# Adding the experts' results to the residual in another shape, and the final norm tile by tile

## The reference, cut to what matters

```
h = x + mixer(rmsnorm(x))                      # 264 rows x 1024
logits = rmsnorm(h) @ w_router + b_router      # top 4 of 32 experts, softmax gates
h = h + sum over the 4 chosen experts e of
        gate_e * (((clip(up)+1) * glu(gate)) @ w_e2[e] + b_e2[e])
y = h * rsqrt(mean(h*h) + 1e-5) * norm_f       # final norm, the outputs y_prompt and y_sample
```

## Time and profile before

| | us |
| --- | --- |
| median of 3 runs (1486.15 to 1487.38) | 1487.25 |
| the profiled execution, whole | 1487.55 |
| its span, first to last instruction | 1485.8 |
| PE busy | 1382.9 (93%) |
| DVE busy | 374.4 (25%) |
| ACT busy | 228.7 (15%) |
| POOL busy | 96.2 (6%) |

### The profile page before, as it was taken

One profiled execution on the slowest core, in us unless ns is written; L12 is line 12 of the kernel. 1 busy time (PEld: TensorE's weight loads), 2 busy tenths in 40 slices (PEclk: granted clock), 3 DMA queues, 4 the chain that ended last, 5 costly groups with the idle time before them and its releaser, 6 DMA issues.

```text
span 1485.8 us, 17919 instructions
## 1 busy us (share of the span) xinstructions
PE 1382.9 (93%) x7365; PEld 707.5 (48%) x7365; DVE 374.4 (25%) x677; ACT 228.7 (15%) x340; POOL 96.2 (6%) x160
## 2 busy tenths in 40 slices
PE   8999989999999988998999989989999899899996
PEld 7667658778888533332433333324333333233331
DVE  3224332532411332122121221221212212211123
ACT  1122222211000421111101111111011111110102
POOL 1122222210000210000000000000000000000000
PEclk9999999999999999999999999999999999999999
DMA  9788867875243469999999999999999999999993
GB/s 373 293 290 277 289 215 281 291 270 208 114 156 135 180 274 428 412 421 431 414 423 430 412 430 422 428 429 421 425 430 427 428 419 421 430 428 418 430 422 136
DMA packets 52063, 518.48 MB, mean 349 GB/s; under 512 B 6167, under 2 KB 6439, under 8 KB 19742
## 3 DMA queue, kind: packets, MB, share of 16 engines
q1 hardware_dynamic: 37370, 469.09, 75.9%
q0 software_dynamic: 12720, 45.14, 9.0%
q10 hardware_dynamic: 1940, 3.78, 0.7%
HBM read 496.35 MB, written 21.67 MB: 349 GB/s over the span
## 4 chain that ended last, share of the span: by engine, by line
PE 84%; DMA 7%; DVE 4%; ACT 3%; issue 1%; POOL 0%; DVEq 0%; SPq 0%; POOLq 0%; ACTq 0%
PE bank L1544 30%; PE bank L1272 17%; PE bank L1578 15%; PE bank L1589 6%; DMA out_ret_sample<-arena 5%; PE bank L1523 4%; PE bank L1315 3%; PE bank L1409 2%; PE bank L1542 1%; ACT arena L862 1%; PE bank L1570 1%; DMA k_kept<-arena 1%; DVE arena L1212 1%; DVE arena L1223 1%; DVE hx L1227 1%
## 5 line engine op out<-in xcount | busy, mean ns | idle before, releaser
L1544 PE MATMUL bank<-ring,arena 128*64 128x512 f32 x2048 | 444.8, 592 | 0.0
L1272 PE MATMUL bank<-arena,ring 128*128 128x264 f32 x1536 | 350.5, 388 | 0.0
L1272 PEld LDWEIGHTS bank<-arena,ring 128*128 128x128 f32 x1536 | 290.3, 190 | 53.5 <-issue 5.0
L1544 PEld LDWEIGHTS bank<-ring,arena 128*64 128x64 f32 x2048 | 143.7, 137 | 283.0 <-issue 277.3
L1578 PE MATMUL bank<-ring,arena 128*64 128x512 f32 x1024 | 225.1, 592 | 0.0
L1578 PEld LDWEIGHTS bank<-ring,arena 128*64 128x64 f32 x1024 | 71.8, 137 | 131.9 <-issue 129.4
L1212 DVE TENSOR_SCALAR arena<-bank 128x512 f32<-128x512 f32 x32 | 22.1, 692 | 396.5 <-PE bank L1544 396.5
L1589 PE MATMUL bank<-arena 128*128 128x512 f32 (+1 forms) x192 | 91.3, 610 | 12.6 <-DVE arena L1223 12.6
L1523 PE MATMUL bank<-arena 128*128 128x128 bf16 x768 | 61.6, 240 | 31.3 <-DVE arena L1204 31.3
L1223 DVE COPY arena<-bank 64x512 f32<-64x512 f32 x32 | 21.9, 683 | 229.0 <-PE bank L1578 229.0
L1523 PEld LDWEIGHTS bank<-arena 128*128 128x128 bf16 x768 | 56.1, 109 | 46.0 <-issue 46.0
(11 more groups left out here) (198 smaller groups left out, 817.7 us busy)
## 6 DMA issues: line engine op xcount, KB each, us to landing
ring<-in_w_pairs SPq DMA_DIRECT2D x192, 2048.0 KB, 15.2
ring<-in_w_mixer SPq DMA_DIRECT2D x60, 1024.0 KB, 9.1
arena<-in_state_ret POOLq DMA_DIRECT2D x32, 512.0 KB, 6.9
out_ret_sample<-arena POOLq DMA_DIRECT2D x32, 512.0 KB, 6.4
arena<-v_decode POOLq DMA_DIRECT2D x32, 256.0 KB, 8.3
out_ret_prompt<-arena ACTq DMA_DIRECT2D x4, 512.0 KB, 5.3
hx<-in_x_prompt SPq DMA_DIRECT2D x2, 512.0 KB, 3.8
v_kept<-arena ACTq DMA_DIRECT2D x2, 512.0 KB, 9.4
```

The lines of the kernel that those rows point to most:

```text
L1272: ins = pe.matmul(bank[:, 0:T], weight(n + k // 4, k % 4)[:, 128 * j:128 * (j + 1)], rhs[:, k, :], start=k == 0, stop=k == KD * groups - 1)
L1544: ins = pe.matmul(out, xgT[:, k, 64 * e:64 * (e + 1)], held(n, 2 * D * (k % W1_KS) + c), start=False, stop=k == KD - 1)
```

## The change

Decode rows are no longer a third tile of 8 rows x 512 columns, added in two halves. Their 1024 columns lie as four groups of 256, group j in partitions 32j to 32j+7 of a new buffer `hs` (128 x 256, zero elsewhere). In the combine four matmuls, each with 32 stationary columns (8 of rows, 24 of zeros), write partitions 32j to 32j+31 of one bank, and one add of 128 x 256 takes them all. The four prompt matmuls follow, each in a bank of its own: 6 for the decode rows, then 7, 0, 1, 2. No combine matmul waits for an add any more. Waits for `added` stand instead before the gather (first two adds) and before the first products of each expert (first four, all five).

```diff
+ADDS = 5
+ADDED = ADDS - 1
+ADD_BANKS = (6, 7, 0, 1, 2)
+ADD_TILES = ((0, 0), (0, 1), (1, 0), (1, 1))
@@ TensorE, combine
-                    for t, n in enumerate(ROWS):
-                        for c in range(2):
-                            if t:
-                                pe.wait_ge(added, 6 * it + (2 * t + c - 1 + ADDED))
-                            pe.matmul(psum[6 + c][0:n, :], pgT[:, 128 * t:128 * t + n], ysb[:, 512 * c:512 * (c + 1)], ...
+                    for j in range(4):
+                        ins = pe.matmul(psum[ADD_BANKS[0]][32 * j:32 * (j + 1), 0:256], pgT[:, LP:LP + 32],
+                                        ysb[:, 256 * j:256 * (j + 1)], start=True, stop=True)
+                    ins.then_inc(combined, 1)
+                    for n, (t, c) in enumerate(ADD_TILES):
+                        pe.matmul(psum[ADD_BANKS[n + 1]][:, :], pgT[:, 128 * t:128 * (t + 1)], ysb[:, 512 * c:512 * (c + 1)], ...
@@ TensorE, gather and first product
-                    pe.wait_ge(added, 6 * it + ADDED)
+                    pe.wait_ge(added, ADDS * it + 1)
+                        pe.wait_ge(added, ADDS * it + (3 + e))     # for e in range(2)
@@ VectorE, adds
+                    v.tensor_tensor(hs[:, :], hs[:, :], psum[ADD_BANKS[0]][:, 0:256], ALU.add).then_inc(added, 1)
+                    for n, (t, c) in enumerate(ADD_TILES):
+                        v.tensor_tensor(hx[:, t, 512 * c:512 * (c + 1)], ..., psum[ADD_BANKS[n + 1]][:, :], ALU.add)
```

The final norm goes by halves of tiles. ScalarE squares and sums `hs`, then each of the four 128 x 512 pieces as its add completes, adding the halves of a row inside the root:

```diff
+            ac.activation(squares3[:, 4, 0:256], hs[:, :], ACT.Square, accum_out=stat[:, 4:5]).then_inc(hs_squared, 1)
+            for n, (t, c) in enumerate(ADD_TILES):
+                ac.activation(squares3[:, n, :], hx[:, t, ...], ACT.Square, accum_out=stat[:, n:n + 1])
+                if c == 0: Identity(scale=1/D, bias=eps) -> stat[5+t]     # mean3
+                else:      Sqrt(scale=1/D, bias=stat[5+t]) -> stat[8+t]   # root3
+                if n == 1: Sqrt of psum[3][:, 0:1] -> stat[7]             # hs_root
```

More of the change, by code:

```diff
@@ L155, in laid_out_experts, with laid_out_tail @@
     return out
+def laid_out_tail(inputs):
+    p = np.arange(128)
+    same_row = (p[:, None] % 32 == p[None, :] % 32).astype(np.float32)
+    return np.concatenate([same_row, np.repeat(inputs["norm_f"].reshape(4, 256), 32, axis=0)], axis=1)
 PROJ_BANKS = 3
@@ L301, in build @@
         rounds_i = sb("rounds_i", [128, 1], I32)
+        hs = sb("hs", [128, D // 4])
         arena = sb("arena", [128, 21700])
@@ L367, in build @@
         acts = view(4096, 2, 512)
-        squares3 = view(1024, TT, D)
+        squares3 = view(1024, 5, D // 2)
+        y_first = view(17148, D)
         actT = view(5120, 2, 512)
         ysb = view(6144, D)
-        pgT = view(7168, T)
+        pgT = view(7168, LP + 32)
+        same_row = view(7456, 128)
+        nfs = view(7584, D // 4)
         n2b = view(15100, D)
@@ L545, in _ @@
                         load_pair(r * PAIRS + pair, pair)
[L547 to L553, removed]
+            sp.wait_ge(hs_out, 1)
+            for j in range(4):
+                sp.dma_start(o["y_sample"][:, 0, 256 * j:256 * (j + 1)], hs[32 * j:32 * j + NS, :]).then_inc(y_out, 16)
+            for c in range(2):
+                sp.wait_ge(y_scaled, c + 1)
+                sp.dma_start(o["y_prompt"][0, 128:256, 512 * c:512 * (c + 1)], hx[:, 1, 512 * c:512 * (c + 1)]).then_inc(y_out, 16)
+            sp.wait_ge(y_out, 16 * 7)
         @block.gpsimd
@@ L654, in _ @@
                 pool.wait_ge(round_done, r + 1)
-            pool.wait_ge(added, 6 * PAIRS * rounds + ADDED)
-            pool.tensor_tensor(y_last[0:NS, :], hx[0:NS, 2, :], nfb[0:NS, :], ALU.mult).then_inc(gained, 1)
+            for c in range(2):
+                pool.wait_ge(added, ADDS * PAIRS * rounds + (c + 1))
+                pool.tensor_tensor(y_first[:, 512 * c:512 * (c + 1)], hx[:, 0, 512 * c:512 * (c + 1)],
+                                   nfb[:, 512 * c:512 * (c + 1)], ALU.mult).then_inc(gained, 1)
         @block.scalar
@@ L844, in _ @@
                 ac.dma_start(o["ret_prompt"][0, 0, h].rearrange("(k p) v -> p k v", p=128), st_kept[i]).then_inc(st_out, 16)
+            ac.wait_ge(hs_zero, 1)
+            for j in range(4):
+                ac.activation(hs[32 * j:32 * j + NS, :], hx[0:NS, 2, 256 * j:256 * (j + 1)], ACT.Copy).then_inc(hs_ready, 1)
             ac.wait_ge(rounds_ready, 1)
@@ L866, in _ @@
             ac.activation(stat[:, 13:14], stat[:, 12:13], ACT.Sqrt)
-            for t, n in enumerate(ROWS):
[L868 to L872, removed]
-            ac.wait_ge(inv3, 1)
-            ac.wait_ge(gained, 1)
-            ac.activation(y_last[0:NS, :], y_last[0:NS, :], ACT.Copy, scale=stat[0:NS, 11:12]).then_inc(y_last_ready, 1)
+            ac.wait_ge(added, ADDS * PAIRS * rounds)
+            ac.activation(squares3[:, 4, 0:256], hs[:, :], ACT.Square, accum_out=stat[:, 4:5]).then_inc(hs_squared, 1)
+            for n, (t, c) in enumerate(ADD_TILES):
+                ac.wait_ge(added, ADDS * PAIRS * rounds + (n + 1))
+                ac.activation(squares3[:, n, :], hx[:, t, 512 * c:512 * (c + 1)], ACT.Square,
+                              accum_out=stat[:, n:n + 1]).then_inc(half_squared, 1)
+                ac.wait_ge(half_squared, n + 1)
+                if c == 0:
+                    ac.activation(stat[:, 5 + t:6 + t], stat[:, n:n + 1], ACT.Identity, scale=1.0 / D,
+                                  bias=stat[:, 15:16]).then_inc(mean3, 1)
+                    ac.wait_ge(mean3, t + 1)
+                else:
+                    ac.activation(stat[:, 8 + t:9 + t], stat[:, n:n + 1], ACT.Sqrt, scale=1.0 / D,
+                                  bias=stat[:, 5 + t:6 + t]).then_inc(root3, 1)
+                if n == 1:
+                    ac.wait_ge(hs_summed, 1)
+                    ac.activation(stat[:, 7:8], psum[3][:, 0:1], ACT.Sqrt, scale=1.0 / D, bias=stat[:, 15:16]).then_inc(hs_root, 1)
+            ac.wait_ge(inv3, 1)
+            for c in range(2):
+                ac.wait_ge(gained, c + 1)
+                ac.activation(y_first[:, 512 * c:512 * (c + 1)], y_first[:, 512 * c:512 * (c + 1)], ACT.Copy,
+                              scale=stat[:, 10:11]).then_inc(y_first_ready, 1)
+            ac.wait_ge(y_first_ready, 2)
+            ac.dma_start(o["y_prompt"][0, 0:128, :], y_first).then_inc(y_out, 16)
             ac.wait_ge(row0_out, 16)
@@ L1223, in _ @@
                         v.tensor_copy(ysb[SLOTS * e:SLOTS * (e + 1), 0:512], psum[4][0:64, :]).then_inc(y_ready, 1)
-                    for t, n in enumerate(ROWS):
-                        for c in range(2):
[L1226 to L1235, removed]
-            for t in range(2):
-                v.scalar_tensor_tensor(hx[:, t, :], hx[:, t, :], stat[:, 9 + t:10 + t], nfb[:, :],
-                                       ALU.mult, ALU.mult).then_inc(y_scaled, 1)
+                    v.wait_ge(hs_ready, 4)
+                    v.wait_ge(combined, ADDS * it + 1)
+                    v.tensor_tensor(hs[:, :], hs[:, :], psum[ADD_BANKS[0]][:, 0:256], ALU.add).then_inc(added, 1)
+                    for n, (t, c) in enumerate(ADD_TILES):
+                        v.wait_ge(combined, ADDS * it + (n + 2))
+                        v.tensor_tensor(hx[:, t, 512 * c:512 * (c + 1)], hx[:, t, 512 * c:512 * (c + 1)],
+                                        psum[ADD_BANKS[n + 1]][:, :], ALU.add).then_inc(added, 1)
+                    v.wait_ge(added, ADDS * it + (ADDS + ADDED))
+            v.wait_ge(tail_in, 16)
+            v.wait_ge(hs_root, 1)
+            v.reciprocal(stat[:, 14:15], stat[:, 7:8]).then_inc(hs_inv, 1)
+            v.wait_ge(hs_inv, 1)
+            v.scalar_tensor_tensor(hs[:, :], hs[:, :], stat[:, 14:15], nfs, ALU.mult, ALU.mult).then_inc(hs_out, 1)
+            for t in range(2):
+                v.wait_ge(root3, t + 1)
+                v.reciprocal(stat[:, 10 + t:11 + t], stat[:, 8 + t:9 + t]).then_inc(inv3, 1)
+            v.wait_ge(inv3, 2)
+            for c in range(2):
+                v.scalar_tensor_tensor(hx[:, 1, 512 * c:512 * (c + 1)], hx[:, 1, 512 * c:512 * (c + 1)], stat[:, 11:12],
+                                       nfb[:, 512 * c:512 * (c + 1)], ALU.mult, ALU.mult).then_inc(y_scaled, 1)
         @block.tensor
@@ L1584, in _ @@
                     pe.wait_ge(y_hi_ready, 2 * it + (2 + PRIMED))
-                    for t, n in enumerate(ROWS):
-                        for c in range(2):
-                            if t:
-                                pe.wait_ge(added, 6 * it + (2 * t + c - 1 + ADDED))
-                            pe.matmul(psum[6 + c][0:n, :], pgT[:, 128 * t:128 * t + n], ysb[:, 512 * c:512 * (c + 1)],
-                                      start=True, stop=True).then_inc(combined, 1)
+                    pe.wait_ge(pad_zero, 1)
+                    for j in range(4):
+                        ins = pe.matmul(psum[ADD_BANKS[0]][32 * j:32 * (j + 1), 0:256], pgT[:, LP:LP + 32],
```

(9 more changed lines are left out.)

15 lines of the change are left out of this document (10 added, 5 removed).

## The result

The changed kernel took 1472.9 us (median of 4 runs, 1469.55 to 1476.54), the kernel before 1487.32 in the runs beside it: ratio 0.9904, 95% interval 0.9877 to 0.9932. Run again on another occasion it took 1472.26 against 1489.1: 0.9879 (0.9858 to 0.9900). The forecast was 1470.5, 16.8 us less than before; measured are 14 and 17. The profiled execution took 1469.55, its span is 1467.7.

A forecast was written before the change was run, and what follows sets the result against it. The prediction took TensorE to bound the kernel, with DMA close behind. Its terms, -14.1 (loop), -2.9 (end) and +0.3 (before the loop), sum to -16.7 us: forecast 1470.5 us, own range 1468 to 1473, 8-in-10 range 1466 to 1476.

The forecast's parts named there:

- The bound: In the expert loop, DMA allows only 14.1 us of the 20.9 us that the shorter combine saves TensorE.
- rival 1: In the loop, DMA doesn't bind and TensorE's 20.9 us count in full: 1463.8 us; chance 6%.
- The wall: In the stream of expert loads, a chunk takes 4.897 us of DMA, so a pair's twelve need 58.8 us.
- The gaps: Pauses in the stream of loads before the change, over 183 landed chunks: 8.4 us in all.
- the lead: At the loop's end, the last chunk landed 5.7 us before TensorE began with it.
- about ten pairs: In the loop, about ten pairs run ahead before TensorE waits for chunks, then some 1.5 us a pair.
- Rival 2: A low clock comes in every pair, giving back 14.7 us, so TensorE binds: 1478.5 us; chance 10%.
- The group: In the combine, the four decode matmuls run together and take 0.6 us, from 0.45 to 2.0.
- Rivals 3 and 4: In the combine, four decode matmuls run in turn: 1484.5 us, chance 4%; or are dearer than that: 1502 us, chance 3%.
- The end: From the last combine's start to the span's end: 13.1 us, a change of -2.9 us, from -4 to -1.
- Ahead of the loop: ScalarE's four added copies before the first pair, mostly hidden under the gather, cost +0.3 us, from 0 to +1.8.
- The sum: Over the whole kernel, the terms give -16.7 us, for a forecast of 1470.5 us.

The follow-up runs named there:

- nobias_after: The changed kernel without the bias product in front of each expert's first product; median 1470.65 us, ratio to the kernel before 0.9859 to 0.9917.
- tail_only: The kernel before with only the final norm tile by tile and the early copies, decode rows normed without experts' sums; median 1486.98 us, ratio 0.9966 to 1.0001.
- loads34_after: The changed kernel with each load of expert weights cut to three quarters of its columns; median 1465.18 us, ratio to the kernel before 0.9819 to 0.9858.

## Why the prediction was right

By its own steps:

- *The bound.* Right; rival 1 fell. The wall of 4.897 us a chunk is 4.894 between landings in every profile with whole loads, however long a load waited in the queue. TensorE's saving of 1.42 us a pair (forecast 1.39) would have been 21.3 us (20.9), and 14.4 arrived at the last combine (14.1). The gaps went entirely and were 9.0 us, not 8.4; the lead shrank from 5.7 us to 0.4 by the same reckoning (1446.91 + 6.89 / 2 against 1449.9), not to 0. These two errors nearly cancel: 9.0 + 5.3 = 14.3. The waits of the matmuls began in the eighth pair; "about ten pairs" was too long, which changes nothing in the sum.
- *The low clock.* Rival 2 counted it as all or nothing. It came in five of fifteen gathers. Steps behind the eighth pair with a low clock took 58.87 us, where the stream needs 58.73. Two such steps in a row were made up by the next, of 58.45. In the last pair it is what sets the end, by 0.14 us. In nobias_after it did come in each of the first eight steps, as rival 2 feared, and still cost nothing: with it a step of that kernel takes 58.06 us, less than the stream's 58.73.
- *The group.* Rivals 3 and 4 fell: 0.57 us with the change of shape, forecast 0.6. Against 0.43 for one matmul of 256 columns that leaves 0.14 for all four starts and the change. The drain at a change of tiling mode, of which the Trainium skill speaks ("TensorEngine Tiling (Array Packing)", Tiling Modes), is within that for the change to the full width. The change into the groups shows no price either: from the start of VectorE's copy to the combine's start it is 0.74 us in both kernels (1469.08 to 1469.82 and 1453.83 to 1454.57).
- *The end.* 2.85 us, forecast 2.9. It divides into 1.4 from the shorter combine and 1.4 from the norm. That the norm's own part depends on what stands in TensorE's queue before its one-column sum came out only in tail_only.
- *Ahead of the loop.* +0.3 was too much. From the last routing copy's end to the seventh issue it was 9.20 us before (527.29 to 536.49) and 9.23 after (526.44 to 535.67). ScalarE's four copies ran from 527.60 to 529.33. They took the place of a pause of 1.62 us before the table load that precedes its first copy of the pair. First the kernel before, then the changed one:

```profile
529.59 1.28 ACT L853 ACT_TABLE_LOAD   x1 [1.62 <-issue]
```

```profile
527.60 1.73 ACT L872 ACTIVATE hs<-hx 8x256 f32<-8x256 f32 x4 [0.48 <-ACT arena L865]
...
530.65 0.60 ACT L880 ACTIVATE arena<-bank 128x512 f32<-128x512 f32 x1
```

Counted from the last routing copy, ScalarE's copy for the first product came 0.57 us later (4.21 instead of 3.64), and it still ended at 531.25, before the first product's start at 532.02. The prediction saw room from 528.00 to 530.93 and had not read the table load in it.

- *The sum.* Rest 17.2 us less in the profiles; forecast 17.0 without the 0.3 ahead of the loop. The profiled execution as a whole took 18.0 us less, since its seventh issue also came 0.8 earlier. The median of the first runs lies 2.4 above the forecast, and the profiled execution was the shortest of the four; so that the forecast came this near to a median was in part luck, since the runs of one kernel spread over 7 us. In the second profile 3.1 of its 3.2 us over the first lie ahead of the stream, a part that no term of mine had let vary; that the other runs differ by the same part was not traced and stays an inference.

## What to carry to other kernels

An engine that never waits for a queue may still be within a few us of it: compare the landings' pace, times the number of transfers, with the loop's own time, and count what buffers and gaps still hold before you price a saving. Beyond that point further savings on the engine were worth nothing here, and lighter transfers helped (loads34_after). Count a saving from start to start of the instructions and not from the duration of a record: the bias products looked like 1.2 us a pair and were worth 0.8. To compare kernels whose first part varies, cut the profiled time at a common event in the middle.

## What the runs showed of the hardware

The pace of the stream did not depend on how much was outstanding: 4.894 us for 2.1 MB with 8 to 25 us from issue to landing. Two loads of 1 MB in place of one of 2 MB lengthened the stream by some 0.08 us each time in the one profile with 16 such pairs (915.6 against 914.2). The landings of its pairs are 58.8 us apart (nearly all 58.81), from the first on, against 58.73 in the changed kernel; a delay by TensorE would show in some pairs and not in all.

Stretches of low clock in the loop are not fixed in number: three to eleven between the profiles. nobias_after had the most (eleven in the loop), at no cost in its rest; nine of them came before its matmuls first waited for a chunk, at 1100.3, so waits for chunks do not explain those. The mean granted clock of an execution is no measure of its time here: 0.981 with a rest of 934.07, 0.991 with 933.88.
